# V's high and low part in one stationary tile: two value matmuls a block instead of three, in an encoder layer on one core

## What is computed

```python
q, k, v = split(h @ w_qkv, 3)                       # 16 heads of 64
z = einsum('bhqd,bhkd->bhqk', q, k) * scale         # blocks of queries, keys up to the block's end
log_stay = where(before, log_sigmoid(-z), 0)
log_pass = cumsum(log_stay, reverse=True) - log_stay
a = where(before, exp(log_sigmoid(z) + log_pass), 0)
o = einsum('bhqk,bhkd->bhqd', a, v)                 # the value product
return o @ w_o
```

## Time and profile before

| | |
|---|---|
| median of 3 runs | 1458.4 us (1454.26, 1458.4, 1458.83) |
| profiled execution | 1454.86 us, its span 1453.1 us |
| TensorE busy | 1381.3 us, 95% of the span, 6848 matmuls |
| weight loads busy | 1153.4 us, 79% |
| VectorE busy | 697.4 us, 48% |
| ScalarE busy | 533.7 us, 37% |
| GpSimd busy | 379.9 us, 26% |
| chain that ended last | TensorE 91%, VectorE 6%, the rest 3% |

### The profile page before, as it was taken

The page is one execution under the profiler, slowest core; times in us unless marked ns, Lnnn a source line. Parts: engine busy times, 40 slices in busy tenths (PEclk is TensorE's granted clock), DMA queues, the critical chain, the costliest instruction groups (busy, mean ns, idle before and its releaser), DMA issues.

```text
span 1453.1 us, 18360 instructions
## 1 busy us (share of the span) xinstructions
PE 1381.3 (95%) x6848; PEld 1153.4 (79%) x6848; DVE 697.4 (48%) x850; ACT 533.7 (37%) x948; POOL 379.9 (26%) x244
## 2 busy tenths in 40 slices
PE   5999999999999986997899999999999999999995
PEld 4788888888888875786688888888888888888884
DVE  6578788787887888232312222313031322223138
ACT  5566666666666664233122111111212121111113
POOL 4111011011011033263053233232413232332326
PEclk9999999999999988998899999999999999999998
DMA  4000000000000013020011111110102111111102
GB/s 188 30 30 21 25 30 30 15 29 29 15 29 29 15 52 123 30 73 29 15 58 59 44 44 43 43 58 29 67 20 72 43 58 43 43 43 43 58 14 117
DMA packets 18336, 66.66 MB, mean 46 GB/s; under 512 B 2032, under 2 KB 2032, under 8 KB 18288
## 3 DMA queue, kind: packets, MB, share of 16 engines
q1 hardware_dynamic: 16560, 59.78, 11.8%
q10 hardware_dynamic: 1728, 6.29, 1.3%
HBM read 61.87 MB, written 4.19 MB: 45 GB/s over the span
## 4 chain that ended last, share of the span: by engine, by line
PE 91%; DVE 6%; ACT 1%; DMA 1%; POOL 0%; issue 0%; POOLq 0%; ACTq 0%; DVEq 0%
PE bank L1134 11%; PE bank L1133 11%; PE bank L1135 11%; PE bank L980 6%; PE bank L982 6%; PE bank L981 6%; PE bank L1181 5%; PE bank L1180 5%; PE bank L1182 5%; PE bank L1084 4%; PE bank L1059 2%; PE bank L1058 2%; PE bank L1056 2%; PE bank L1104 2%; PE bank L1103 2%; PE bank L1029 2%
## 5 line engine op out<-in xcount | busy, mean ns | idle before, releaser
L681 POOL TENSOR_TENSOR w_lo<-raw,w_hi 128x1024 fp32r<-128x1024 f32 x89 | 216.7, 2439 | 770.4 <-ACT w_hi L421 770.2
L1133 PE MATMUL bank<-hnT_hi,w_hi 128*128 128x512 f32 x704 | 277.3, 394 | 2.9 <-DVE hnT_lo L782 2.9
L1134 PE MATMUL bank<-hnT_lo,w_hi 128*128 128x512 f32 x704 | 278.5, 396 | 0.0
L1135 PE MATMUL bank<-hnT_hi,w_lo 128*128 128x512 f32 x704 | 276.0, 392 | 0.0
L421 ACT ACTIVATE w_hi<-raw 128x1024 fp32r<-128x1024 f32 x89 | 93.4, 1060 | 404.6 <-PE bank L1135 353.4
L913 DVE TENSOR_TENSOR sg<-bank,sg 128x512 f32<-128x512 f32 x44 | 30.4, 692 | 437.7 <-ACT sg L614 437.7
L856 DVE TENSOR_TENSOR_SCAN stay<-stay,diag_one 128x256 f32<-128x256 f32 (+7 forms) x128 | 196.2, 1533 | 3.8 <-ACT stay L541 3.8
L927 DVE TENSOR_TENSOR y<-bank,y 128x512 f32<-128x512 f32 x176 | 119.3, 690 | 94.4 <-PE bank L1182 93.1
L1133 PEld LDWEIGHTS bank<-hnT_hi,w_hi 128*128 128x128 f32 x704 | 132.8, 189 | 34.7 <-DVE hnT_lo L782 3.5
L1135 PEld LDWEIGHTS bank<-hnT_hi,w_lo 128*128 128x128 f32 x704 | 132.9, 189 | 29.9
L429 ACT ACTIVATE AT_hi<-bank 128x512 fp32r<-128x512 f32 (+1 forms) x160 | 89.0, 556 | 183.2 <-PE bank L1084 182.5
(11 more groups left out here) (100 smaller groups left out, 2134.4 us busy)
## 6 DMA issues: line engine op xcount, KB each, us to landing
raw<-in_units SPq DMA_DIRECT2D x98, 512.0 KB, 3.3
acc<-in_x SPq DMA_DIRECT2D x8, 512.0 KB, 8.7
x_in<-in_x ACTq DMA_DIRECT2D x8, 512.0 KB, 3.4
out<-y SPq DMA_DIRECT2D x7, 512.0 KB, 2.6
g_pre_s<-in_mix_pre ACTq DMA_DIRECT2D x1, 512.0 KB, 5.5
g_post_t<-in_mix_post ACTq DMA_DIRECT2D x1, 512.0 KB, 4.2
g_ffn_t<-in_ffn_pre ACTq DMA_DIRECT2D x1, 512.0 KB, 3.7
g_out<-in_ffn_post ACTq DMA_DIRECT2D x1, 512.0 KB, 3.7
```

Source lines behind the costliest of these rows:

```text
L681: nc.gpsimd.tensor_tensor(w_lo[slot], raw[:, raw_slot, :], w_hi[slot].bitcast(F32), ALU.subtract).then_inc(w_ready, 1)
L1133: nc.tensor.matmul(bank_ap, wh, hnT_hi[:, kt, cols], start=(kt == 0), stop=False)
L1134: nc.tensor.matmul(bank_ap, wh, hnT_lo[:, kt, cols], start=False, stop=False)
L1135: mm = nc.tensor.matmul(bank_ap, wl, hnT_hi[:, kt, cols], start=False, stop=(kt == KT - 1))
```

## The change

**V's tile** becomes [P, 8 blocks of keys, 4, 64]: head 0 high, head 0 low, head 1 low, head 1 high. A stationary tile is now (high, low) for head 0 and (low, high) for head 1, with no zeros in it.

**The matmuls** of a block become two: that tile x AT high and that tile x AT low. Half of the output's partitions hold the products with V high, the other half those with V low, so the product low x low is formed too. Since all partitions are used by one head, a bank now belongs to a head and not to X or Y, and is filled by one group.

**The end of a group.** The two halves have to be added. ScalarE's `o_move` copies the half with V low to the head's place in `acc` (64 partitions x 512), in slots 14, 19, 4 and 9; VectorE's `o_add` adds the bank's other half to it one slot later, in slots 15, 0, 5 and 10. A new semaphore `o_moved` lies between them; `o_done` now counts additions, 4 a pair. TensorE waits for the addition of the group two before, and the copy of an output tile waits for the last pair's two X (or all four) additions. The tail has 11 slots. The clearing of V's zeros at the start goes.

```diff
-O_SLOT = {19: 0, 9: 1}
-TAIL_SLOTS = 10
+O_COPY = {14: (0, 0), 19: (0, 1), 4: (-1, 2), 9: (-1, 3)}
+O_ADD = {15: (0, 0), 0: (-1, 1), 5: (-1, 2), 10: (-1, 3)}
+TAIL_SLOTS = 11
+TAIL_O = {0: 0, 3: 1}
...
-                V = alloc(qk, "V", [P, NT, 2, 3, HD], F32R)
+                V = alloc(qk, "V", [P, NT, 4, HD], F32R)
...
+        def values(o_p, group):
+            h, x = GROUPS[group]
+            return (o_p.rearrange("q (g n) -> q g n", n=2 * P)[OWN[h], 0:4:3, :] if x == "X"
+                    else o_p[OWN[h], 2 * P:6 * P])
+        def values_bank(group, part):
+            h, x = GROUPS[group]
+            b = OB[h][part, :]
+            return b.rearrange("q (g n) -> q g n", n=2 * P) if x == "X" else b
...
-            def o_copy(p, half_q):
-                act.wait_ge(av_done, SLOTS * p + (SLOTS if half_q else SLOTS // 2))
+            def o_move(p, group):
+                act.wait_ge(av_done, SLOTS * p + GROUP * (group + 1))
...
+                nc.scalar.activation(values(o_p, group), values_bank(group, OTHER[GROUPS[group][0]]),
+                                     ACT.Copy).then_inc(o_moved, 1)
             def o_hi_copy(t):
-                act.wait_ge(o_done, 2 * PAIRS - (1 if t in ROWS["X"] else 0))
+                act.wait_ge(o_done, 4 * PAIRS - (2 if t in ROWS["X"] else 0))
...
-            nc.vector.memset(V[:, :, :, 1, :].bitcast(F32), 0.0).then_inc(zeros, 1)
...
+            def o_add(p, group):
+                dve.wait_ge(o_moved, 4 * p + group + 1)
...
+                nc.vector.tensor_tensor(o, values_bank(group, OWN[GROUPS[group][0]]), o, ALU.add).then_inc(o_done, 1)
...
-                        if z % (SLOTS // 2) == 0 and not (first or isinstance(p, int) and p == 0):
-                            pe.wait_ge(o_done, 2 * (p - 1) + half_q + 1)
+                        group = 4 * (p - (s < T_LAG + AV_LAG)) + z // GROUP
+                        if z % GROUP == 0 and not (isinstance(group, int) and group < 2):
+                            pe.wait_ge(o_done, group - 1)
...
-                            nc.tensor.matmul(dst, vl, hi, start=(z % (SLOTS // 2) == 0 and m == 0), stop=False,
+                            nc.tensor.matmul(dst, v, hi, start=(z % GROUP == 0 and m == 0), stop=False,
                                              skip_group_check=True)
-                            nc.tensor.matmul(dst, vh, hi, start=False, stop=False, skip_group_check=True)
-                            mm = nc.tensor.matmul(dst, vh, lo, start=False,
-                                                  stop=(z % (SLOTS // 2) == SLOTS // 2 - 1 and m == 1),
+                            mm = nc.tensor.matmul(dst, v, lo, start=False, stop=(z % GROUP == GROUP - 1 and m == 1),
                                                   skip_group_check=True)
```

More of the change, by code:

```diff
@@ L365, in encoder_layer @@
         av_done = sem("av_done")
+        o_moved = sem("o_moved")
         o_done = sem("o_done")
@@ L549, in step @@
                         qk_hi(step_units(p, "q")[0], "q", 1 - par, 0, ACCB[0])
-                    if O_SLOT.get(s) == 0 and not tail:
-                        o_copy(p, 0)
-                    if O_SLOT.get(s) == 1 and not first:
-                        o_copy(p - 1, 1)
+                    if s in O_COPY and not (first and O_COPY[s][0] < 0):
+                        dp, group = O_COPY[s]
+                        o_move(p + dp, group)
                     if proj and s in SPLIT_SLOT:
@@ L558, in step @@
                         split_wo(WO_SPLIT[s])
-                    if tail and s in (0, 3):
-                        o_hi_copy(s // 3)
+                    if tail and s in TAIL_O:
+                        o_hi_copy(TAIL_O[s])
             step(0, 0, first=True)
@@ L827, in projections @@
                     qk_lo(4 * p + 4 + 3, "q", 1 - par, 0, ACCB[0])
+            def o_add(p, group):
+                dve.wait_ge(o_moved, 4 * p + group + 1)
+                o_p = acc[:, p, :] if isinstance(p, int) else acc[:, bass.ds(p, 1), :].rearrange("q a n -> q (a n)")
+                o = values(o_p, group)
+                nc.vector.tensor_tensor(o, values_bank(group, OWN[GROUPS[group][0]]), o, ALU.add).then_inc(o_done, 1)
             def o_lo_sub(t):
@@ L841, in step @@
                         if kind == "v" and not tail:
-                            t_lo_sub(g, V[:, 4 * at:4 * at + 4, 1, 0:3:2, :],
+                            t_lo_sub(g, V[:, 4 * at:4 * at + 4, 1:3, :],
                                      TB[(n - T_LAG) % 2][:, :].rearrange("p (k h c) -> p k h c", k=4, h=2),
-                                     V[:, 4 * at:4 * at + 4, 0, 0:3:2, :])
+                                     V[:, 4 * at:4 * at + 4, 0:4:3, :])
                         elif kind == "a" and not (first and s < T_LAG) and not (tail and s >= T_LAG):
@@ L862, in step @@
                         projections(p, par, s, first, proj)
-                    if tail and s in (0, 3):
-                        o_lo_sub(s // 3)
+                    if s in O_ADD and not (first and O_ADD[s][0] < 0):
+                        dp, group = O_ADD[s]
+                        o_add(p + dp, group)
+                    if tail and s in TAIL_O:
+                        o_lo_sub(TAIL_O[s])
             step(0, 0, first=True)
@@ L995, in _ @@
             pe.wait_ge(consts, 5)
-            pe.wait_ge(zeros, 4)
+            pe.wait_ge(zeros, 3)
             for t in range(NT + 1):
```

14 lines of the change are left out of this document (3 added, 11 removed).

## The result

The changed kernel takes 1435.6 us (median of 4 runs, 1431.4 to 1438.1) against 1457.4 (4 runs, 1454.3 to 1458.8): ratio 0.985, 95% interval 0.983 to 0.987. It is 1.5% faster, inside the range on record and 8.6 us above the 1427 forecast. The direction and the mechanism held. Of the 30.8 us of the sum, 21.8 arrived in the medians. The profiled execution of the changed kernel took 1431.4 us (span 1429.6), the profiled one of before 1454.9: 23.5 us apart, where the sum said 30.8.

The account below looks back on a forecast made before the run. TensorE was taken to bound the attention loop, VectorE the last pair. Saved 33.5 us less 2.7 lost gave 30.8 off the profiled 1454.9, 1424.1, shifted by 3.5 to the median: 1427, range 1419 to 1440.

Parts of the forecast that it names:

- TensorE sets the loop, 0.233 us a slot: Attention loop: TensorE is the limit, and four value matmuls instead of six save 0.233 us in each slot.
- The estimate of 98 ns: Value matmuls: 98 ns for one of 256 columns by the skill's figures, making the 33.5 us gain 28.2.
- Additions and copies cost nothing in the loop: Loop: VectorE at 54.7 and ScalarE at about 43.3 of 60.3 us a pair stay under TensorE, so cost nothing.
- The margin at slot 1, 0.38 us: Slot 1, the tightest place: AT_lo's margin before its value matmuls falls from 1.54 to 0.38 us, so TensorE doesn't wait.
- rival (b): Loop: the 0.38 us margin is missing, TensorE waits 0.5 to 1.5 us a step, clock may fall; 1431 to 1449, chance 0.15.
- Last pair and hand-over, 2.7 us lost: Last pair: two additions cost 1.4 us, the chain to the output projection 1.8, less 0.5 of idle gained.
- The tail, 1.6 us gained: Tail between 577 and 601 us: seven slots with shorter value passes save 1.6 us.
- Work that the change doesn't touch, nothing: Start and everything behind the tail: no difference between the two kernels, 0 us.
- (c): Loop: VectorE's idle time is latency of a loop, so additions lengthen each step by 2.8 us; 1477, chance 0.03.
- (e): Value passes: a removed matmul gives back only 0.09 us, as it takes a short one along; 1434, chance 0.02.
- (d): Last pair: additions run in GpSimd's shadow, collisions fall more kindly, idle is gained whole; 1417 to 1422, chance 0.07.
- rival (a): The forecast itself: TensorE keeps the attention stage as its limit; 1422 to 1432, chance 0.73.

Follow-up runs that it names:

- e10: Changed kernel with 54 waits and 13 unread matmuls in front, one copy moved from slot 19 to 18 and its addition from slot 0 to 19: 1423.5 us.
- e3: Changed kernel with a third value matmul put back in each block (AT high multiplied twice): 1460.5 us, ratio 1.0031 to the kernel before.
- e4: Changed kernel with one copy moved from slot 19 to 18 and its addition from slot 0 to 19: 1433.0 us, ratio 0.985.
- e8: Changed kernel with 13 unread matmuls filling the wait before the first scores and 54 instructions of waits in front: 1424.0 us, ratio 0.977.
- e9: Kernel before with only the 13 unread matmuls filling the wait before the first scores: 1456.0 us, ratio 0.9992.
- e12: Changed kernel with the 13 unread matmuls and 460 waits (230 instructions) ahead of TensorE's first work: 1442.3 us, ratio 0.991.
- e1: The changed kernel run again, unchanged: 1433.2 us, ratio 0.9845 to the kernel before.
- e7: Kernel before with 128 waits (64 instructions) ahead of TensorE's first work: 1457.5 us, ratio 1.000.

## Why the prediction was right, point by point

- **TensorE sets the loop, 0.233 us a slot.** Right. 0.46 and 0.47 us for four matmuls; steps of 60.31 (e10) against 64.95, so 4.64 / 20 = 0.232. The estimate of 98 ns, worked out in a side sentence from the figures of the Trainium skill ("TensorE: Matmul & The Clock Gate", section "Back-to-back issue gap"), would have made it 3.9 us a step; the rows of before decided rightly.
- **Additions and copies cost nothing in the loop.** Right, shown by e3: 64.95 us a step with three passes. An addition measures 0.66 to 0.70 us, 54.8 us of VectorE a pair.
- **The margin at slot 1, 0.38 us.** Right: 0.43. But the sentence after it, that slot 15 is next, was wrong. Slot 2 went from 3.05 us to 0.05, because the prediction moved VectorE's work by the addition's length without looking at what GpSimd does beside it. Two rows had shown how long a collision is; this step failed because the prediction priced it in the last pair only. Cost by e4 and e10 against after and e8: 0.1 to 0.2 us a step. That is rival (b)'s mechanism at another place and at well under its 0.5 to 1.5 us.
- **Last pair and hand-over, 2.7 us lost.** Right in size: 3.1 in the first pair of profiles. From slot 6 of the last pair to the output projection, e9 takes 50.5 us and e8 53.5: 3.0. The chain is the one named. In the changed kernel, VectorE, ScalarE, VectorE and TensorE:

```profile
545.13 0.69 DVE L845 TENSOR_TENSOR acc<-bank,acc 64x512 f32<-64x512 f32 x1
546.95 1.23 DVE L850 TENSOR_TENSOR o_lo_t<-acc,o_hi_t 128x1024 fp32r<-128x1024 f32 x1 [1.12 <-ACT o_hi_t L516]
```

```profile
545.86 1.06 ACT L516 ACTIVATE o_hi_t<-acc 128x1024 fp32r<-128x1024 f32 x1 [6.52 <-DVE acc L845]
```

```profile
548.32 0.76 PE L1050 MATMUL bank<-hnT_hi,o_hi_t 128*128 128x512 f32 x1 [6.68 <-DVE o_lo_t L850]
```

  Addition at 545.13, o_hi at 545.86, o_lo at 546.95: 545.13 to 546.95 is 1.82 us, the 1.8 of the prediction. ScalarE had nothing else to do for 6.52 us. The prediction left open whether an addition beside GpSimd runs at its own length (the Trainium skill, "SBUF — State Buffer", section "Who interferes with whom"). In the changed kernel's last pair none fell beside a subtract of GpSimd's. In e12 one did, GpSimd's row first:

```profile
540.72 2.74 POOL L722 TENSOR_TENSOR hnT_lo<-raw,hnT_hi 128x1024 fp32r<-128x1024 f32 x1 [0.89 <-ACT hnT_hi L502]
```

```profile
541.16 0.67 DVE L845 TENSOR_TENSOR acc<-bank,acc 64x512 f32<-64x512 f32 x1
541.76 0.54 DVE L794 TENSOR_TENSOR AT_lo<-bank,AT_hi 128x384 fp32r<-128x384 f32 x1
542.22 1.65 DVE L878 TENSOR_TENSOR A<-A,stay 128x384 f32<-128x384 f32 x1
```

  The addition and the subtract behind it, each with one input in PSUM, kept their length (0.67 and 0.54), and the multiply of A, both of whose inputs are in SBUF, took 1.65 us instead of 0.55. Nor does any AT_lo of 512 columns that falls beside GpSimd in the changed kernel get longer: 0.69 us at most, as without it. (A multiply that had begun at 540.57, just before GpSimd's subtract, kept its 0.66.) The trace agrees with the rule, and the plain 0.70 was the right price.
- **The tail, 1.6 us gained.** 0.8 in the first pair of profiles, 1.3 in e8 against e9. The size was right and the clock took the rest. Before the tail's first value matmul stand twelve matmuls of the output projection. In before they took 4.47 us (572.82 to 577.29), eight of them at half clock. In the changed kernel all twelve ran at half clock, 548.32 to 553.58:

```profile
553.58 0.28 PE L1076 MATMUL bank<-AT_hi,V 128*128 128x128 f32 x1
```

  That is 5.26 us, and the 0.8 us more is what was missing. In e8 and e9 they took 4.53 and 4.20.
- **Work that the change doesn't touch, nothing.** This was the step that missed most. The prediction took the profiled execution of before as the state that both kernels would be in. It was the favourable one: full clock after the 3.24 us wait, no fetches in the loop. The change shifted the medians by 21.8 us instead of 30.8, and both profiled executions of the changed kernel carry a burden: 3.3 us for the start's clock and 1.8 behind the tail (the first), or 7.5 us in the loop for the jumps and the clock behind them (e1). Which of them the other executions carry, their times alone don't tell. The 3.5 us by which the prediction moved the profiled time to the median stood, by e9, for the first of these in before, without its cause being known. e8 against e9 comes near the sum: 29.5 us in the stages that the change touches, 31.0 in all.
- **Rivals.** (c) fell with e3, (e) with the 0.23 us a slot. (d)'s gain did not come. Of (b), the place is another and the price far smaller. By the sum's own terms (e) should have read 1435 and not 1434. The 1435.6 lies outside the 1422 to 1432 of rival (a), the forecast, and inside the range only by the part that was put there for (b), whose mechanism did not make the difference. That the range held is so in part luck: the 8.6 us come from the clock and the fetches, which none of the five named, and in what shares they do is open.

## What to carry to other kernels

When TensorE is the bound and a loop gets shorter, the per-slot price from distances between starts can be good to a few per cent, as it was here; what took a quarter of it back sat outside the slots. To find it, look in the profile at the instruction queue's packets of both kernels, and at "issue" waits behind a loop's jump, before looking for a lost semaphore. And when an operation is put in on VectorE, lay GpSimd's long operations beside the shifted timeline too: the margin that goes may be the one two operations further on.

## What the runs showed of the hardware

- The queue "q8 instruction" moves packets of some 16 KB, and its times and counts fit TensorE's code (inferred). A loop whose turn holds some 710 matmuls with as many weight loads (2132 in three turns) was either left alone by the queue in its later turns (23 or 24 packets in all) or fetched anew in each (41 or 42). With the fetches came 0.9 us at two jumps in e7 and 6.7 in e1. A matmul kernel that nothing else holds up may be held up by its own program.
- The same wait of 3.24 us was followed by a full clock in three profiles and by a mean of 0.83 to 0.91 over 20 us in six. Within one kernel that was worth 3.6 us (e1 against the first profile). 13 matmuls in it, 3 us of TensorE's time that was idle, left the clock full in all five profiles that had them, in both kernels. 16 matmuls ahead of a longer wait, with 3.9 us of idle time left over, did not raise the clock behind it.
- A subtract or addition of VectorE's with one input in PSUM kept its length beside GpSimd (0.67 us in e12); a multiply with both inputs in SBUF went from 0.55 to 2.75 us.
- Waits that are already fulfilled are not free on TensorE: 460 of them moved its first work from 9.69 to 26.14 us; 108 of them, that fit in the 9.7 us it waits there anyway, moved nothing.
